# A mixture-of-experts stage on one core: another order of turns between single large experts and pairs of small ones

## The chip, the cores and the metric

The kernel runs on one core of a Trainium2 chip. The metric is device time in microseconds (us), the median of several executions. It has 2298.35 us before the change (three executions, 2296.97 to 2299.94).

## What is computed

Two transformer-like blocks over 256 tokens of width 1024. All but the last part stays as it is. The change touches only the last mixture of experts: 8 experts, each a SwiGLU of inner width 2816, two experts for each token.

```python
N_EXPERTS_2, TOP_K, D_EXPERT = 8, 2, 2816

def swiglu(t, w_gate, w_up, w_down):
    return (jax.nn.silu(t @ w_gate) * (t @ w_up)) @ w_down

def moe_swiglu(h, w_router, w_gate, w_up, w_down):
    t = h.reshape(bsz * seq, d)
    ...
    gates = jnp.sum(jax.nn.one_hot(top_idx, N_EXPERTS_2, dtype=jnp.float32) * top_w[..., None], axis=1)
    out = jnp.zeros_like(t)
    for e in range(N_EXPERTS_2):
        out = out + gates[:, e:e + 1].astype(t.dtype) * swiglu(t, w_gate[e], w_up[e], w_down[e])
    return out.reshape(bsz, seq, d)
```

## The kernel before

At run time the experts are ranked by how many tokens they have. Ranks 0 to 3 are the large experts: each is worked on alone, with up to 128 tokens in its rows. Ranks 4 and 5 make one pair and ranks 6 and 7 the other; each pair shares the 128 rows, 64 for either expert. A large expert is item 0, 1, 2 or 3 of the table `STEPS`; the pairs are items 4 and 5. `HEAVY = 4` parts the two kinds.

An item has four steps. Steps 0, 1 and 2 are chunks of the inner width (1024, 1024 and 768 columns): the gate product, the up product, and silu(gate) times up. Step `OUT` (3) is the product with the down weights. Each engine has its own instruction stream and walks through `STEPS` in the same order (`ranked_pe`, `ranked_act`, `ranked_experts_dve`, and `sync`, which issues the loads), so the one table sets the order of everything.

All weights come once from HBM, in units of two rows of the contraction index: 128 x 2048 float32, 1.049 MB, or three quarters of that in step 2. They go into the ring `fine`, which has 8 slots. SyncE loads unit u as soon as unit u - 8 is released (`Ring.load`, L139), strictly in order of `STEPS`. A step needs these units:

- large expert: 8 in steps 0 and 1, 8 of three quarters in step 2 (6 full ones in bytes), 11 in `OUT`
- pair: twice as many (16, 16, 16 of three quarters, 22), and always two slots together, one of each expert.

The two kinds use a unit differently. A large expert's weights are split into a high and a low part in fp32r: ScalarE casts to `w_hi` (L192, `make_hi`), VectorE subtracts to `w_lo` (L202, `make_lo`), in parts of 1024 columns with four buffers (`PARTS`), and TensorE makes three products of each (L263 to L265). The slot is released when the last `w_lo` of the unit is made, up to four parts ahead of TensorE. A pair's weights are multiplied straight from the slot in float32 (L2476 for gate and up, L2532 for down), and both slots are released when TensorE has done with them.

Between the products lie a few other steps. `mid_pe` (L2269) turns the middle result of the step before, behind the gate product of the next step. `scatter_pe` (L252) adds a finished item's rows back to the tokens; it waits for the chain `y_gated` (VectorE, L2418), `ysb_hi` (ScalarE, L2351), `ysb_lo` (VectorE, L2424). `heavy_end` says how far ScalarE and VectorE may split ahead: to the end of the uninterrupted run of steps of large experts.

Of the kernel before, what the change touches and what calls it, by code (L numbers as in the profile page):

```python
# [301 lines left out]
def row_parts(n, kt=KD):  # L302
# [13 lines left out]
HEAVY = 4  # L316
RANKS = {0: (0,), 1: (1,), 2: (2,), 3: (3,), 4: (4, 5), 5: (6, 7)}
OUT = 3
STEPS = ((0, 0), (0, 1), (4, 0), (0, 2), (0, OUT), (4, 1), (1, 0), (1, 1), (4, 2), (1, 2), (1, OUT), (4, OUT),
         (2, 0), (2, 1), (5, 0), (2, 2), (2, OUT), (5, 1), (3, 0), (3, 1), (5, 2), (3, 2), (3, OUT), (5, OUT))  # L320
INS = [step for step in STEPS if step[1] != OUT]
OUTS = [i for i, ch in STEPS if ch == OUT]

# [6 lines left out]
def heavy_after(i, ch):  # L330

    n = STEPS.index((i, ch)) + 1
    return next((step for step in STEPS[n:] if step[0] < HEAVY), None)


def heavy_end(i, ch):

    n = STEPS.index((i, ch))
    while n + 1 < len(STEPS) and STEPS[n + 1][0] < HEAVY:
        n += 1  # L340
# [3743 lines left out]
```

## Time and profile before

| what | before |
|---|---|
| median of three executions | 2298.35 us |
| profiled execution, its own time | 2297.53 us |
| its span in the trace | 2295.7 us |
| TensorE busy | 1971.2 us (86%) |
| VectorE busy, ScalarE busy | 1088.6 us, 852.2 us |
| weights of the last experts (264 units of 1.049 MB) | 277 MB |

The last experts take about the last 690 us of the span. In this text a "run" is a series of steps of large experts with no pair between them. DMA rates are those of all 16 engines together. TensorE's rows overlap each other by pipelining, so its busy share is no measure of how near it is to its peak.

### The profile page before, as it was taken

The page shows a single profiled execution, that of the slowest core. Times are in us where ns is not written, and L with a number is a line of the kernel's source. Part 1 is how long each engine was busy: PE and PEld are TensorE (multiplying, and loading weights), DVE is VectorE, ACT ScalarE, POOL GpSimd, SP SyncE. Part 2 cuts the span into 40 slices and gives each one's busy share as a digit, 9 for nine tenths or more (in the row PEclk, how much of TensorE's full clock was granted, in tenths as well). Part 3 has the DMA queues.
Part 4 walks back from the last instruction along what each step waited for, and adds up shares of the span by engine and source line. Part 5 has one row for each costly group of instructions (what it writes and reads, how often), then busy time and mean ns, then how long its engine had stood idle before and what let it go on. Part 6 is the DMA issues. An engine that isn't in the chain of part 4 may idle for free.

```text
span 2295.7 us, 29235 instructions
## 1 busy us (share of the span) xinstructions
PE 1971.2 (86%) x12057; PEld 1404.6 (61%) x12057; DVE 1088.6 (47%) x1665; ACT 852.2 (37%) x1153; POOL 43.7 (2%) x109
## 2 busy tenths in 40 slices
PE   6989997996666666698999999999989998999996
PEld 6968776762211211256899898878575674674672
DVE  3845555431111110223555477866484572573571
ACT  4432345310000000234444357855363452463460
POOL 0010200000000000000000000000000000000000
PEclk9989999999777888899999999998999999999999
DMA  8463562579999999849455544405999999999996
GB/s 266 174 220 111 200 233 75 208 296 394 409 409 409 409 409 409 326 174 370 159 183 184 201 130 160 167 5 227 384 390 387 390 408 409 389 407 409 381 408 274
DMA packets 227524, 663.02 MB, mean 289 GB/s; under 512 B 20101, under 2 KB 28841, under 8 KB 227125
## 3 DMA queue, kind: packets, MB, share of 16 engines
q1 hardware_dynamic: 219628, 652.92, 74.4%
q10 hardware_dynamic: 7752, 8.11, 1.2%
q8 instruction: 99, 1.62, 0.3%
q14 instruction: 45, 0.36, 0.1%
HBM read 659.90 MB, written 1.10 MB: 288 GB/s over the span
## 4 chain that ended last, share of the span: by engine, by line
PE 53%; DMA 23%; DVE 13%; ACT 7%; issue 3%; POOL 0%; ACTq 0%; SPq 0%; DVEq 0%; POOLq 0%
PE psum L263 11%; PE psum L265 11%; PE psum L264 11%; PE psum L252 6%; DMA ring<-in_w_expert_down 5%; DMA ring<-in_w_expert_up 5%; DMA ring<-in_w_expert_gate 5%; PE psum L2476 4%; DMA ring<-in_moe_w_gate 3%; DVE w_lo L202 3%; PE psum L2773 2%; ACT w_hi L192 2%; DMA ring<-in_moe_w_down 2%; PE psum L2532 2%; PE psum L1184 1%
## 5 line engine op out<-in xcount | busy, mean ns | idle before, releaser
L202 DVE TENSOR_TENSOR w_lo<-ring,w_hi 128x1024 fp32r<-128x1024 f32 (+1 forms) x498 | 579.6, 1187 | 415.0 <-ACT w_hi L192 406.6
L192 ACT CAST w_hi<-ring 128x1024 fp32r<-128x1024 f32 (+1 forms) x498 | 501.0, 1020 | 390.4 <-PE psum L265 286.5
L2773 PE MATMUL psum<-ring,hT 128*32 128x512 f32 x960 | 158.7, 796 | 104.3 <-DMA ring<-in_w_expert_gate 58.7
L2773 PEld LDWEIGHTS psum<-ring,hT 128*32 128x32 f32 x960 | 31.2, 129 | 224.7 <-issue 100.9
L2476 PE MATMUL psum<-ring,xg_pair 128*64 128x512 f32 (+1 forms) x768 | 156.5, 559 | 13.3 <-DMA ring<-in_moe_w_up 13.3
L263 PE MATMUL psum<-w_hi,xg_hi 128*128 128x512 f32 (+1 forms) x384 | 148.1, 386 | 17.5 <-DVE w_lo L202 17.4
L2379 DVE TENSOR_TENSOR x<-x,psum 128x1024 f32<-128x1024 f32 x26 | 31.2, 1219 | 253.1 <-PE psum L252 253.1
L265 PE MATMUL psum<-w_lo,xg_hi 128*128 128x512 f32 (+1 forms) x384 | 145.8, 380 | 0.0
L264 PE MATMUL psum<-w_hi,xg_lo 128*128 128x512 f32 (+1 forms) x384 | 145.8, 380 | 0.0
L2476 PEld LDWEIGHTS psum<-ring,xg_pair 128*64 128x64 f32 x768 | 55.5, 137 | 108.9 <-issue 105.8
L2795 PE MATMUL psum<-ring,midT 128*32 128x512 f32 x480 | 69.8, 716 | 41.6 <-DMA ring<-in_w_expert_down 41.1
L263 PE MATMUL psum<-h_f_hi,w_hi 128*128 128x256 f32 x352 | 100.6, 286 | 1.5 <-DVE h_f_lo L895 1.5
L264 PE MATMUL psum<-h_f_hi,w_lo 128*128 128x256 f32 x352 | 100.4, 285 | 0.0
L265 PE MATMUL psum<-h_f_lo,w_hi 128*128 128x256 f32 x352 | 100.3, 285 | 0.0
L263 PEld LDWEIGHTS psum<-w_hi,xg_hi 128*128 128x128 f32 x384 | 73.5, 191 | 39.0 <-DVE w_lo L202 13.4
L2532 PE MATMUL psum<-ring,midT 128*64 128x512 f32 x352 | 79.3, 596 | 12.2 <-DMA ring<-in_moe_w_down 12.2
L265 PEld LDWEIGHTS psum<-w_lo,xg_hi 128*128 128x128 f32 x384 | 73.2, 191 | 14.5
L264 PEld LDWEIGHTS psum<-w_hi,xg_lo 128*128 128x128 f32 x384 | 73.4, 191 | 13.9
L259 PE MATMUL psum<-ident 128*128 128x128 f32 x582 | 73.5, 285 | 0.0
L263 PE MATMUL psum<-w_hi,midT_hi 128*128 128x512 f32 x176 | 70.3, 399 | 3.0 <-DVE w_lo L202 3.0
L259 PEld LDWEIGHTS psum<-ident 128*128 128x128 f32 x582 | 71.1, 201 | 2.1 <-issue 1.6
L263 PE MATMUL psum<-h_mix_hi,w_hi 128*128 128x256 f32 x224 | 63.1, 282 | 7.8 <-DVE w_lo L202 7.8
(694 smaller groups left out, 3676.7 us busy)
## 6 DMA issues: line engine op xcount, KB each, us to landing
ring<-in_moe_w_down SPq DMA_DIRECT2D x88, 1024.0 KB, 14.2
ring<-in_w_expert_gate SPq DMA_DIRECT2D x32, 2048.0 KB, 17.6
ring<-in_moe_w_gate SPq DMA_DIRECT2D x64, 1024.0 KB, 12.9
ring<-in_moe_w_up SPq DMA_DIRECT2D x64, 1024.0 KB, 12.7
ring<-in_w_expert_down SPq DMA_DIRECT2D x30, 2048.0 KB, 17.0
ring<-in_w_expert_up SPq DMA_DIRECT2D x28, 2048.0 KB, 17.4
ring<-in_ada_w SPq DMA_DIRECT2D x24, 2048.0 KB, 11.7
ring<-in_moe_w_gate SPq DMA_DIRECT2D x32, 768.0 KB, 11.1
```

The source lines that it names most:

```text
L192: a.copy(self.buffers(n, src.shape)[0], src).then_inc(*self.hi_made.up())
L202: v.tensor_tensor(lo, src, hi.bitcast(F32), SUB).then_inc(*self.lo_made.up())
L252: ins = p.matmul(o, l, r, start=n == 0, stop=n == len(terms) - 1)
L259: p.matmul(o[:, 0:P], constant[:, :], constant[:, :], start=True, stop=True)
L263: p.matmul(o, l[0], r[0], start=start, stop=False)
L264: p.matmul(o, l[1], r[0], start=False, stop=False)
L265: return p.matmul(o, l[0], r[1], start=False, stop=stop)
L2379: v.tensor_tensor(M.acc[:, t, :], M.acc[:, t, :], run.banks.of(st.name, "scatter", i, t), ADD).then_inc(*st.dve.up("acc", i, t))
L2476: ins = p.matmul(ps[r, cut], moe2.xg_pair[:, i - HEAVY, k0 + k, r], w[side][:, k, cut], start=k0 + k == 0, stop=k0 + k == KD - 1)
L2532: ins = p.matmul(ps[r, cut], M.midT[:, k0 + k, r], w[side][:, k, cut], start=first, stop=last)
L2773: ins = p.matmul(ps[slots_of(j), g * 512:(g + 1) * 512], M.xg[:, 2 * q + k, slots_of(j)], w[:, j, k, :], start=2 * q + k == 0, stop=2 * q ...
L2795: ins = p.matmul(ps[slots_of(j), cut], M.midT[:, q, slots_of(j)], w[:, j, cut], start=q == 0, stop=q == 3)
```

## The change

Only the last two thirds of the table `STEPS` change. Nothing is added or removed; the same products, splits and loads come in another order.

```diff
-STEPS = ((0, 0), (0, 1), (4, 0), (0, 2), (0, OUT), (4, 1), (1, 0), (1, 1), (4, 2), (1, 2), (1, OUT), (4, OUT),
-         (2, 0), (2, 1), (5, 0), (2, 2), (2, OUT), (5, 1), (3, 0), (3, 1), (5, 2), (3, 2), (3, OUT), (5, OUT))
+STEPS = ((0, 0), (0, 1), (4, 0), (0, 2), (0, OUT), (4, 1), (1, 0), (4, 2), (1, 1), (1, 2), (1, OUT), (4, OUT),
+         (2, 0), (5, 0), (2, 1), (5, 1), (2, 2), (2, OUT), (3, 0), (5, 2), (3, 1), (3, 2), (3, OUT), (5, OUT))
```

Up to (1, 0) both orders are the same, and the order in which the items end (`OUTS`) stays as well. In ScalarE's stream, at the third pair step (4, 2), `w_hi` is the split of a large expert's weights, `hT` the silu, and `midT` the turned middle result (`midT_hi` for a large expert). The difference reads:

```order
 L2582 COPY midT<-psum 128x1024
-L192 CAST w_hi<-ring 128x1024 x16
-L2602 ACTIVATE hT<-psum 128x1024
-L2582 CAST midT_hi<-psum 128x1024
 L192 CAST w_hi<-ring 128x1024 x4
 L2602 ACTIVATE hT<-psum 128x768
 L2582 CAST midT_hi<-psum 128x1024
+L192 CAST w_hi<-ring 128x1024 x12
+L2602 ACTIVATE hT<-psum 128x1024
+L2582 COPY midT<-psum 128x768
```

The silu of the pair's chunk (128x768) now follows one chunk of expert 1, and the second chunk of expert 1 comes behind it.

The second place is the end of expert 2 in VectorE's stream. `total` is `y_gated`, `x` the addition to the tokens, `selg` the selection of the next item's rows, `ada_row` the middle result. Before, the end of expert 2 is followed by a pair, (5, 1):

```order
L202 TENSOR_TENSOR w_lo<-ring,w_hi 128x1024 x16
L2418 SCALAR_TENSOR_TENSOR total<-psum,slot_gate,gate_b 128x1024
L2424 TENSOR_TENSOR ysb_lo<-total,ysb_hi 128x1024
L2379 TENSOR_TENSOR x<-x,psum 128x1024 x2
L202 TENSOR_TENSOR w_lo<-ring,w_hi 128x1024
L2674 TENSOR_TENSOR ada_row<-hT,psum 128x1024
L202 TENSOR_TENSOR w_lo<-ring,w_hi 128x1024 x3
L2648 TENSOR_SCALAR selg<-slots,ranked 128x128 x2
```

Now it is followed by a large expert's chunk, (3, 0), with the pair (5, 2) behind that:

```order
L202 TENSOR_TENSOR w_lo<-ring,w_hi 128x1024 x20
L2418 SCALAR_TENSOR_TENSOR total<-psum,slot_gate,gate_b 128x1024
L2424 TENSOR_TENSOR ysb_lo<-total,ysb_hi 128x1024
L2648 TENSOR_SCALAR selg<-slots,ranked 128x128 x2
L202 TENSOR_TENSOR w_lo<-ring,w_hi 128x1024 x8
L2379 TENSOR_TENSOR x<-x,psum 128x1024 x2
L202 TENSOR_TENSOR w_lo<-ring,w_hi 128x1024 x4
```

Four more parts are split ahead (20, not 16), and the chain of `y_gated` and `ysb_lo` now stands between splits that TensorE needs at once.

## Rows read from the trace of the kernel before

**Rows 1.** The page: span, and busy time of each engine

```profile
span 2295.7 us, 29235 instructions
PE 1971.2 (86%) x12057; PEld 1404.6 (61%) x12057; DVE 1088.6 (47%) x1665; ACT 852.2 (37%) x1153; POOL 43.7 (2%) x109
```

**Rows 2.** Windows of the last stage: busy us by engine, clock, DMA share, GB/s

```profile
1705.00:1740.00 35.00, 35.00 (x157) 21.87 (x157) 19.73 (x17) 13.96 (x14) 0.00 (x0) 1.00 0.91 343
1740.00:1800.00 60.00, 56.85 (x256) 38.25 (x253) 40.06 (x36) 35.64 (x35) 0.00 (x0) 1.00 1.03 409
1800.00:1820.00 20.00, 20.00 (x114) 11.50 (x114) 5.42 (x6) 3.93 (x5) 0.00 (x0) 1.00 0.95 361
1820.00:1925.00 105.00, 98.94 (x488) 61.27 (x486) 52.06 (x58) 42.19 (x50) 0.00 (x0) 1.00 1.03 407
...
1985.00:2000.00 15.00, 15.00 (x71) 5.80 (x71) 1.22 (x1) 0.00 (x0) 0.00 (x0) 1.00 0.85 332
...
2065.00:2100.00 35.00, 31.21 (x139) 12.71 (x137) 5.99 (x5) 2.07 (x2) 0.00 (x0) 1.00 1.03 409
...
2150.00:2165.00 15.00, 15.00 (x89) 7.55 (x89) 1.22 (x1) 1.78 (x2) 0.00 (x0) 1.00 0.87 313
```

**Rows 3.** Waits of SyncE's DMA queue, 1650 to 2296: total us, times, longest

```profile
SPq L139 <- DVE w_lo L202: 270.9, 124, 6.1
```

**Rows 4.** Chain that ended last, 1590 to 2296: start, us, what

```profile
1650.78 13.31 DMA ring<-in_moe_w_up
...
1727.07 13.88 PE psum L2476 x64
...
1757.27 1.05 ACT w_hi L192
...
1761.89 0.50 PE psum L263
...
1807.21 10.47 PE psum L2476 x64
...
1830.30 0.84 ACT w_hi L192
...
1833.91 0.50 PE psum L263
...
1883.33 7.02 PE psum L2532 x32
...
1932.20 1.05 ACT w_hi L192
...
1939.22 0.50 PE psum L263
...
1939.99 0.43 PE psum L265
...
1987.02 13.88 PE psum L2476 x64
...
2015.70 0.84 ACT w_hi L192
...
2019.74 0.50 PE psum L263
...
2069.38 13.88 PE psum L2476 x64
...
2102.49 1.05 ACT w_hi L192
...
2107.11 0.51 PE psum L263
...
2152.50 10.47 PE psum L2476 x64
```

**Rows 5.** VectorE's timeline at the end of expert 2

```profile
2069.42 1.28 DVE L2418 SCALAR_TENSOR_TENSOR total<-psum,slot_gate,gate_b 128x1024 f32<-128x1024 f32 x1 [3.28 <-PE psum L265]
2071.81 1.22 DVE L2424 TENSOR_TENSOR ysb_lo<-total,ysb_hi 128x1024 fp32r<-128x1024 f32 x1 [1.11 <-ACT ysb_hi L2351]
```

## Prediction

> **What bounds the kernel now.** I read the page first. TensorE is busy 86% of the span [rows 1], which invites the thought that TensorE is the limit. The windows of the last stage correct that: DMA moves 407 to 409 GB/s wherever nothing holds it up, with its share at its top value [rows 2]. At that rate a unit of 1.049 MB takes 1.049 / 0.409 = 2.56 us, so the 264 units of the last experts need 676 us of a stage of about 690. The stage is bound by transfers, with TensorE close behind, and the only time that another order can win or lose is time in which DMA has nothing to fetch because all 8 slots are taken.
>
> The windows show such stretches, always where a pair's step begins: 343 GB/s in 1705 to 1740, 361 in 1800 to 1820, 332 in 1985 to 2000, 313 in 2150 to 2165 [rows 2]. In lost time, length x (1 - rate / 409), these are 5.6, 2.3, 2.8 and 3.5 us. The first lies ahead of the changed part. The other three, at (4, 2), (5, 0) and (5, 2), sum to 8.7 us (I add the unrounded values). They are what the change can remove at the very most: 0.38% of the time.
>
> Why there? The chain of waits gives the pace of each kind [rows 4]. A large expert's chunk takes TensorE 22.7 us: two of them lie between 2107.11 and 2152.50. Its loads take 8 x 2.56 = 20.5. So DMA gains 2.2 us on TensorE in each chunk, plus the head start at a run's beginning. On a pair the sign is the other way: 64 rows of L2476 take 13.88 us for four double units, 3.5 us each, against 5.1 us of loading. A pair's step lets TensorE catch up and wait. SyncE's queue waits for `w_lo` 270.9 us in all, 124 times [rows 3], but most of that is an ordinary full queue with loads in flight; only the windows tell when it cost anything.
>
> **A rule for the stall.** Take as zero the time when the first unit of a run starts to load (its landing in rows 4 minus its own transfer). DMA runs dry when it has loaded the run and the first 8 units of the pair behind it. It gets a slot again when TensorE has done the pair's first double unit. The margin M is the second time minus the first. From rows 4:
>
> - (4, 2): zero at 1757.27 - 2.56 = 1754.7. DMA dry at + 16 x 2.56 + 8 x 1.92 = 1811.1. TensorE starts the pair at 1807.2, + 2.6 for three-quarter units. M = -1.3, measured stall 2.3.
> - (5, 0): zero 1932.20 - 2.56 = 1929.6, dry at + 24 x 2.56 = 1991.1, TensorE 1987.0 + 3.5. M = -0.6, stall 2.8.
> - (5, 2): zero 2099.9, dry at 2156.3, TensorE 2152.5 + 2.6. M = -1.2, stall 3.5.
> - (4, 1): zero 1650.78 + 13.31 = 1664.1, dry at + 25 x 2.56 = 1728.1, TensorE 1727.1 + 3.5. M = +2.5, stall 5.6.
> - (4, OUT): zero 1830.30 - 1.92 = 1828.4, dry at 1892.4, TensorE 1883.3 + 3.5. M = -5.6, no stall: 407 GB/s [rows 2].
> - (5, 1): zero 2013.8, dry at 2077.8, TensorE 2069.4 + 3.5. M = -4.9, no stall: 409 GB/s [rows 2].
>
> The stall is M + k with k of 3.1 to 4.7, and zero where that is negative. I read k as the issue of new loads, the time until they deliver at full rate, and the thinning out of the last ones; the rows give only its sum. I take k = 3.5, and 4.7 for (5, 2), which showed it. The Trainium skill ("DMA: Bandwidth & Descriptors", section "Anatomy of one DMA") gives a fixed part of about 2.0 us for each transfer; taken alone as k it would be an estimate about 1.5 us smaller at each stall, and the measured k speaks for more than that.
>
> **The change, place by place.** The new runs are: (1, 0) alone; (1, 1), (1, 2), (1, OUT); (2, 0) alone; (2, 1) alone; (2, 2), (2, OUT), (3, 0); (3, 1), (3, 2), (3, OUT). In units the old ones were 16, 17, 16, 17, 16, 17; the new ones are 8, 25, 8, 8, 25, 25. Runs are halved where they were short, and three of them grow to 25.
>
> - *(4, 2) behind (1, 0).* TensorE's start was +52.5 and comes 22.7 earlier, at +29.8, + 2.6; dry at 20.5 + 15.4 = 35.9. M = -3.5, and with k = 3.5 nothing is left; with k = 4.7 it is 1.2, the bound. Gain 2.3.
> - *(4, OUT) behind 25 units.* First matmul of the run: the first unit's 2.56 plus the 4.6 from landing to matmul (1757.27 to 1761.89). Then 22.7 for (1, 1) and 49.4 for (1, 2) and (1, OUT) (1833.91 to 1883.33). TensorE starts the pair at +79.3, + 3.5. Dry at 20.5 + 43.6 + 20.5 = 84.6. M = -1.8, stall 1.7. Loss 1.7; bounds 0 and 3.
> - *(5, 0) behind (2, 0).* Before, run start to pair start was 57.4; without (2, 1) it is 34.7, + 3.5; dry at 41.0. M = -2.8, stall 0.7. Gain 2.1.
> - *(5, 1) behind (2, 1).* First matmul +7.2, chunk 22.7, + 3.5 = 33.4 against 41.0. M = -7.6: no stall, and none before.
> - *(5, 2) behind (2, 2), (2, OUT), (3, 0).* First matmul +5.9 (2013.8 to 2019.74); (2, 2) and (2, OUT) 49.6 (2019.74 to 2069.38). Then (3, 0): 22.7, about 1.0 more for the scatter in the place of a turned middle, and a new wait. For the first time a large expert's `OUT` is followed by a large expert's chunk. Four parts are split ahead; that covers TensorE for 4 x 1.4 = 5.6 us (22.7 / 16 a part). But the fourth can be cast only when the last part of `OUT` is used: its two steps take about 2.2, then `y_gated` 1.28, `ysb_hi` about 1.1, `ysb_lo` 1.22 [rows 5], `selg` about 0.6, and the fifth `w_lo` 1.2, in all 7.6. Two us are not covered. Were the fourth part early, nothing would be; that is the lower bound. So (3, 0) takes 25.7, the pair starts at +81.2, + 2.6; dry at 15.4 + 28.2 + 20.5 + 15.4 = 79.5. M = +4.3, and with k = 4.7 the stall is 9.0 against 3.5 now. Loss 5.5; bounds 2 (no uncovered wait, k 3.1: 5.4) and 7.
> - *(5, OUT) behind 25 units.* As (4, OUT): loss 1.7; bounds 0 and 3.
>
> Sum: -2.3 + 1.7 - 2.1 + 5.5 + 1.7 = +4.5 us. The end itself does not move otherwise: (5, OUT) is a pair's step and ends on its last transfer in both orders. Against the profiled execution (own time 2297.53, 1.8 above the span) it gives 2302.0; its own time is 0.8 below the median, so measured medians should stand at 2298.35 + 4.5, about 2302.9.
>
> **The rivals.** A measurement of this kernel can tell 0.2%, 4.6 us, from no change; the forecast lies at that edge.
>
> *Within the noise (24%).* The long runs cost their lead and no more: no uncovered wait at (3, 0), k at its low end, (4, OUT) and (5, OUT) hidden as today. Stalls 5.4 instead of 8.7: -3.3, about 2295. For it: VectorE waits 3.28 us for TensorE ahead of `y_gated` [rows 5], so it has time in hand. Against: those four parts are capped by the buffers.
>
> *Faster (11%).* One mechanism: the stall comes from two whole chunks ahead of a pair, not from the length of a run. Runs that end in `OUT` stand ahead of (4, OUT) and (5, 1) without a stall, and if that holds for 25 units the stalls at (4, 2) and (5, 0) go with nothing in their place: -5.1, or -8.7 (2289.6) if (5, 2) is free too. It decides when the three long runs together add under 0.5 us. Against it is (4, 1): a run with `OUT`, M above zero, 5.6 us lost.
>
> *Much slower (13%).* TensorE loses its clock more often. At 1939.99 a matmul takes 0.43 us [rows 4], after the gap from the landing at 1932.20; at 22.7 / 96 = 0.24 us a matmul normally, some nine such rows cost about 1.8 us. After the shorter gap at 1757 the chain goes on at full pace, and the windows show 1.00. In the new order pairs follow each other sooner, so TensorE waits for loads through more of each pair's step. Were each of three new run starts to cost 1.8 us and pass it on to the stall behind it, the time would be 2308.3. The Trainium skill ("TensorE: Matmul & The Clock Gate", section "HAM oscillation — how this bites in real kernels") describes just such a kernel, half clock after each wait for DMA. The trace agrees for the long gap at 1932 only.
>
> **How the numbers follow.** The forecast's own case (52%) reaches from +1.5 to +8, where the bounds above put it: 2300 to 2306. The range must take in the quiet case and most of the slow one: 2295.5 to 2309. Chances: faster by over 0.2%, the 11% and a sliver of the quiet case, 12%. Slower by over 0.2%, all 13% and, since +4.5 lies at the edge, rather more than half of my main case, 33%: 46%. The rest, 42%, is within 0.2%.
>
> **What would show it.** In the windows of the changed kernel DMA stays above 400 GB/s at the starts of (4, 2) and (5, 1). It falls well below at (5, 2), for about 9 us in lost time, which is the largest loss behind (1, 0). Small losses stand at (4, OUT) and (5, OUT). Between (2, OUT) and (3, 0) TensorE waits about 2 us for `w_lo` about 5 us into the chunk. It would be wrong if (5, 2) starts with a ring that still has loads in flight, or if rows of 0.43 us come at the new run starts.

## The result, and the profile after

The changed kernel takes 2303.94 us (median of 9 executions, 2299.69 to 2307.91); the kernel before took 2297.47 in the same series (9 executions). The ratio is 1.0029, with a 95% interval of 1.0020 to 1.0037: slower by about 6.5 us. The forecast was 2302.9 with a range of 2295.5 to 2309.0, or 4.5 us slower.

The time before the last experts varies by several us from one execution to the next: TensorE's first pair starts between 1632.95 and 1641.17 us in the profiles of this study. So spans say little here, and the profiled execution of the changed kernel (2299.69 us) is also the fastest of its nine. I compare the stage itself, from the start of TensorE's first pair, (4, 0), to the end of its last matmul of weights. These four rows are the two ends in the chain of waits, of the kernel before and then of the changed one; the columns are start, us, what.

```profile
1636.38 13.91 PE psum L2476 x64
...
2276.37 3.67 PE psum L2532 x16
```

```profile
1632.95 13.88 PE psum L2476 x64
...
2278.54 3.67 PE psum L2532 x16
```

The stage takes 2280.04 - 1636.38 = 643.7 us before and 2282.21 - 1632.95 = 649.3 after: 5.6 us more, which is the change of the median within its interval. From here on "the stage" is this stretch.

The windows of the changed kernel answer to [rows 2]. Last column: GB/s; the one ahead of it: DMA's busy share.

```profile
1780.00:1800.00 20.00, 18.26 (x111) 8.14 (x111) 2.44 (x2) 1.82 (x2) 0.00 (x0) 1.00 1.03 401
1800.00:1880.00 80.00, 75.92 (x362) 60.31 (x359) 64.99 (x61) 56.26 (x59) 0.00 (x0) 0.98 1.03 407
1880.00:1910.00 30.00, 30.00 (x144) 13.21 (x144) 7.48 (x15) 3.19 (x5) 0.00 (x0) 1.00 0.95 369
...
1960.00:1980.00 20.00, 20.00 (x96) 7.93 (x96) 2.44 (x2) 2.03 (x2) 0.00 (x0) 1.00 0.98 383
1980.00:2045.00 65.00, 57.65 (x260) 30.36 (x256) 22.35 (x19) 20.00 (x20) 0.00 (x0) 1.00 1.03 409
...
2115.00:2140.00 25.00, 25.00 (x121) 17.59 (x121) 15.96 (x14) 9.78 (x10) 0.00 (x0) 1.00 0.77 270
...
2230.00:2255.00 25.00, 25.00 (x114) 11.33 (x114) 8.15 (x12) 1.64 (x2) 0.00 (x0) 1.00 0.95 375
```

The reader is to look for the rates under 407 and turn each into lost time, length x (1 - rate / 409):

| pair's step | before | forecast | after |
|---|---|---|---|
| (4, 2) | 2.3 | 0 | 0.4 |
| (4, OUT) | 0 | 1.7 | 2.9 |
| (5, 0) | 2.8 | 0.7 | 1.3 |
| (5, 1) | 0 | 0 | 0 |
| (5, 2) | 3.5 | 9.0 | 8.5 |
| (5, OUT) | 0 | 1.7 | 2.1 |
| sum, us | 8.7 | 13.1 | 15.2 |

The difference, 6.5 us, is as large as the change of the median; the stage of the two profiled executions grew by 5.6. Added up over the whole stage, in windows of 5 us, the lost time goes from 24.8 to 30.2 us, which is 5.4 more and fits the stage. That the six places alone give just the 6.5 of the median is partly luck.

The chain of the changed kernel answers to [rows 4]. These are the run starts and the pair starts behind them.

```profile
1753.81 1.05 ACT w_hi L192
...
1758.43 0.50 PE psum L263
...
1780.51 10.47 PE psum L2476 x64
...
1805.59 1.05 ACT w_hi L192
...
1809.94 0.79 PE psum L263
1810.74 0.43 PE psum L264
...
1883.53 7.02 PE psum L2532 x32
...
1929.38 1.05 ACT w_hi L192
...
1962.26 13.88 PE psum L2476 x64
...
2133.56 10.47 PE psum L2476 x64
2144.03 1.02 PE psum L2269 x8
...
2157.17 1.05 ACT w_hi L192
...
2235.10 7.02 PE psum L2532 x32
```

At (4, OUT) the run's first load lands at 1805.59, so the zero of the margin is 1803.0. DMA's dry point is 1803.0 + 84.6 = 1887.6, TensorE gives the first slots back at 1883.53 + 3.5: M = -0.6, and the loss of 2.9 means k = 3.5. The other places are read in the same way below.

The new wait at the junction of (2, OUT) and (3, 0) is the one row that the old trace could not have. First TensorE's row of the timeline, then VectorE's.

```profile
2114.68 0.47 PE L263 MATMUL psum<-w_hi,xg_hi 128*128 128x512 f32 x1 [2.07 <-DVE w_lo L202]
```

```profile
2106.78 2.57 DVE L202 TENSOR_TENSOR w_lo<-ring,w_hi 128x1024 fp32r<-128x1024 f32 x2 [0.23 <-ACT w_hi L192]
2109.27 1.28 DVE L2418 SCALAR_TENSOR_TENSOR total<-psum,slot_gate,gate_b 128x1024 f32<-128x1024 f32 x1
2111.66 1.23 DVE L2424 TENSOR_TENSOR ysb_lo<-total,ysb_hi 128x1024 fp32r<-128x1024 f32 x1 [1.11 <-ACT ysb_hi L2351]
2112.80 0.60 DVE L2648 TENSOR_SCALAR selg<-slots,ranked 128x128 f32<-128x128 f32 x2
2113.31 6.90 DVE L202 TENSOR_TENSOR w_lo<-ring,w_hi 128x1024 fp32r<-128x1024 f32 x6
```

VectorE makes no `w_lo` between 2109.35 and 2113.31, so the fifth part is ready only at about 2114.5. TensorE took up the first of its four parts in store at 2107.0, and they last to 2112.61; from there it waits.

### The profile page after: what moved, and what is told of

The parts are those of the page before. It is cut to its first block, busy times and chain, and to the rows that moved or that the text cites. A ratio compares the mean times of both kernels' runs of the same rounds, so it can differ in the third digit from the quotient of the medians.

```text
span 2297.9 us, 29235 instructions
## 1 busy us (share of the span) xinstructions
PE 1957.1 (85%) x12057; PEld 1402.4 (61%) x12057; DVE 1088.9 (47%) x1665; ACT 852.4 (37%) x1153; POOL 43.5 (2%) x109
## 4 chain that ended last, share of the span: by engine, by line
PE 55%; DMA 22%; DVE 13%; ACT 7%; issue 3%; POOL 0%; ACTq 0%; SPq 0%; DVEq 0%; POOLq 0%
PE psum L263 11%; PE psum L264 11%; PE psum L265 11%; PE psum L252 6%; DMA ring<-in_w_expert_down 5%; DMA ring<-in_w_expert_up 5%; DMA ring<-in_w_expert_gate 5%; PE psum L2476 4%; DMA ring<-in_moe_w_gate 3%; DVE w_lo L202 3%; PE psum L2773 2%; PE psum L2532 2%; ACT w_hi L192 2%; DVE xbc L983 1%; PE psum L1184 1%
## 5 line engine op out<-in xcount | busy, mean ns | idle before, releaser
L2773 PE MATMUL psum<-ring,hT 128*32 128x512 f32 x960 | 146.1, 740 | 117.9 <-DMA ring<-in_w_expert_gate 64.6
L2476 PE MATMUL psum<-ring,xg_pair 128*64 128x512 f32 (+1 forms) x768 | 156.9, 560 | 16.7 <-DMA ring<-in_moe_w_up 14.6
L2773 PEld LDWEIGHTS psum<-ring,hT 128*32 128x32 f32 x960 | 30.2, 125 | 227.0 <-issue 89.0
## 6 DMA issues: line engine op xcount, KB each, us to landing
ring<-in_moe_w_gate SPq DMA_DIRECT2D x32, 768.0 KB, 13.1
```

Source lines behind the costliest of these rows:

```text
L2476: ins = p.matmul(ps[r, cut], moe2.xg_pair[:, i - HEAVY, k0 + k, r], w[side][:, k, cut], start=k0 + k == 0, stop=k0 + k == KD - 1)
L2773: ins = p.matmul(ps[slots_of(j), g * 512:(g + 1) * 512], M.xg[:, 2 * q + k, slots_of(j)], w[:, j, k, :], start=2 * q + k == 0, stop=2 * q ...
```

## Experiments

Each kernel was timed in the same series as the kernel before, and its ratio is to that one. Where a diff shows the table `STEPS`, the line taken away is that of the changed kernel.

**Only expert 1 reordered.** It asks whether the three groups cost alike.

```diff
-         (2, 0), (5, 0), (2, 1), (5, 1), (2, 2), (2, OUT), (3, 0), (5, 2), (3, 1), (3, 2), (3, OUT), (5, OUT))
+         (2, 0), (2, 1), (5, 0), (2, 2), (2, OUT), (5, 1), (3, 0), (3, 1), (5, 2), (3, 2), (3, OUT), (5, OUT))
```

> Only expert 1 gets the new order, (1, 0), (4, 2), (1, 1), (1, 2), (1, OUT), (4, OUT); experts 2 and 3 keep the old one. Theory of the margin: the stall at (4, 2) goes from 2.3 to about 0.4 us, one of about 3.0 appears at (4, OUT), the stalls at (5, 0) and (5, 2) stay at 2.8 and 3.5; in sum about +1 us against the kernel before. Rival, each run of 25 units costs a like share of what the whole change cost (6.5 us over three such runs): +2.2 us. Rival, the loss has nothing to do with this group: 0 or a gain of 2.

Measured: 2296.20 us against 2297.13, ratio 0.9995 (0.9984 to 1.0005). The stage takes 643.6 us, as before. Two windows of its trace, at (4, 2) and at (4, OUT):

```profile
1800.00:1820.00 20.00, 14.91 (x75) 8.84 (x76) 8.15 (x8) 7.42 (x8) 0.00 (x0) 1.00 1.03 406
1885.00:1905.00 20.00, 20.00 (x95) 8.95 (x95) 7.20 (x14) 2.12 (x3) 0.00 (x0) 1.00 0.95 367
```

The loss of 2.3 at (4, 2) is gone, and 2.1 have come at (4, OUT). The group is neutral. A like share for every long run is refuted: 2.2 us, ratio 1.0010, lies beyond the interval.

**Only experts 2 and 3 reordered.**

```diff
-STEPS = (..., (1, 0), (4, 2), (1, 1), (1, 2), (1, OUT), (4, OUT),
+STEPS = (..., (1, 0), (1, 1), (4, 2), (1, 2), (1, OUT), (4, OUT),
```

> Only experts 2 and 3 get the new order. Theory of the margin: (5, 0) 1.3 us of lost transfer time instead of 2.8, (5, 2) 8.5 instead of 3.5, (5, OUT) 2.1 instead of 0, (4, 2) still 2.3: in sum about +5.5 us against the kernel before. Rival, equal share for each run of 25 units: +4.3 us. Whichever, the windows should show one large loss, ahead of and at (5, 2).

Measured: 2303.58 us against 2297.13, ratio 1.0028 (1.0017 to 1.0039), stage 649.0. This half makes the whole loss. Its own windows show 305 GB/s in 2115 to 2155, 10.2 us at (5, 2), where 8.5 was forecast: one large loss, and not a like share for each long run. Seven matmuls at 0.43 us (half clock; 0.23 us at full clock) stand in the run ahead of it, behind the new wait, which the changed kernel's profiled execution does not have there.

```profile
2115.00:2155.00 40.00, 37.91 (x181) 25.56 (x181) 22.21 (x22) 16.25 (x17) 0.00 (x0) 0.96 0.85 305
```

**The new wait taken away.** In the changed kernel one more part is split between the halves of the chain.

```diff
             for k0 in range(0, M.n_k, M.kout):
                 lo_after(v, i, OUT, out_unit(i, k0))
+            if heavy_end(i, OUT) != (i, OUT):
+                y_gated_dve(v, run2, i, run2.multiplied(out_unit(i)))
+                fine_split.make_lo(v, fine_split.end(out_unit(i)) + PARTS + 1)
+                y_lo_dve(v, run2, i)
+                return
...
             for k0 in range(0, M.n_k, M.kout):
                 hi_after(a, i, OUT, out_unit(i, k0))
+            if heavy_end(i, OUT) != (i, OUT):
+                fine_split.make_hi(a, fine_split.end(out_unit(i)) + PARTS + 1)
```

> The changed kernel, but at the end of expert 2 a fifth part is cast and subtracted between the two halves of the chain y_gated, ysb_hi, ysb_lo. Theory: TensorE's wait of 2.1 us inside (3, 0) goes, (5, 2) starts 2.1 us earlier and its stall falls from 8.5 to about 6.4: 2 us faster than the changed kernel, some 4.4 slower than before. Rival, the wait is hidden because DMA has loads in flight then: the wait goes and the stall at (5, 2) and the time stay as in the changed kernel.

Measured: 2301.01 us against 2297.13, ratio 1.0011 (1.0001 to 1.0022); stage 647.6, 1.7 less than the changed kernel. TensorE's waits in 2100 to 2125:

```profile
PE psum L263 <- DVE w_lo L202: 0.6, 1, 0.6
```

2.07 us of waiting have become 0.6, and at (5, 2) the windows show 321 GB/s in 2115 to 2150, a loss of 7.5 instead of 8.5, where 6.4 was forecast. The wait does pass on to the end, so the rival that it is hidden falls. Between 1.0 us (the windows) and 1.7 us (the stage) of the loss were this wait. The intervals of this kernel and the changed one overlap, so it is the trace that carries this, not the medians.

**The pair ahead of (3, 0).** No junction of two large experts, but a run of 33 units.

```diff
-         ... (2, 2), (2, OUT), (3, 0), (5, 2), (3, 1), (3, 2), (3, OUT), (5, OUT))
+         ... (2, 2), (2, OUT), (5, 2), (3, 0), (3, 1), (3, 2), (3, OUT), (5, OUT))
```

> The changed order with (5, 2) moved ahead of (3, 0): runs of 8, 25, 8, 8, 17 and 33 units. It takes away the junction of a large expert's down product with a large expert's chunk. Theory of the margin: (5, 2) behind 17 units has M = 5.9 + 49.6 + 2.6 - 59.0 = -0.9 and loses 2.6 to 3.8 us; (5, OUT) behind 33 units has M = 6.9 + 45.4 + 49.4 + 3.5 - 105.1 = +0.1 and loses 3.2 to 4.8 us; with 3.4 at expert 1 and 1.3 at (5, 0) about 11.7 in sum, 3 us slower than before and 3 faster than the changed kernel. Rival, a run's length alone sets the loss: 33 units lose more than the 8.5 us of 25, and the kernel is 7 us or more slower than before.

Measured: 2297.88 us against 2297.13, ratio 1.0003 (0.9994 to 1.0013); stage 646.7, 3.0 more than before and 2.6 less than the changed kernel. The windows at (5, 2) and at (5, OUT):

```profile
2100.00:2125.00 25.00, 25.00 (x127) 15.96 (x126) 11.54 (x10) 8.73 (x9) 0.00 (x0) 1.00 0.90 340
...
2210.00:2255.00 45.00, 44.25 (x199) 28.02 (x199) 28.21 (x30) 18.26 (x18) 0.00 (x0) 1.00 0.96 369
```

They lose 4.2 and 4.4 us; the forecasts were 2.6 to 3.8, which was a little too low, and 3.2 to 4.8. The longest run of all loses half of what 25 units lost ahead of (5, 2), so length alone does not set the loss. The median is 2 us better than the stage makes one expect.

**An order with one short run.** It keeps the short run (2, 0), without a junction of two large experts.

```diff
-STEPS = (..., (1, 0), (4, 2), (1, 1), (1, 2), (1, OUT), (4, OUT),
-         (2, 0), (5, 0), (2, 1), (5, 1), (2, 2), (2, OUT), (3, 0), (5, 2), (3, 1), (3, 2), (3, OUT), (5, OUT))
+STEPS = (..., (1, 0), (1, 1), (4, 2), (1, 2), (1, OUT), (4, OUT),
+         (2, 0), (5, 0), (2, 1), (2, 2), (2, OUT), (5, 1), (3, 0), (5, 2), (3, 1), (3, 2), (3, OUT), (5, OUT))
```

> An order between the two: (1, 0), (1, 1), (4, 2), (1, 2), (1, OUT), (4, OUT), (2, 0), (5, 0), (2, 1), (2, 2), (2, OUT), (5, 1), (3, 0), (5, 2), (3, 1), (3, 2), (3, OUT), (5, OUT): runs of 16, 17, 8, 25, 8, 25 units, and no large expert's chunk behind a large expert's down product. Theory: stalls of 2.3 at (4, 2), 1.3 at (5, 0), 1.7 to 3 at (5, 1), 0.4 at (5, 2), 2 at (5, OUT), in sum about 8 against 8.7: the same as before within 0.1%. Rival, each run of 25 units costs 2.2 us net: 4 us slower than before.

Measured: 2292.79 us against 2298.70, ratio 0.9979 (0.9966 to 0.9991): faster than before. The stage takes 640.5, 3.2 less. Its two runs of 25 units stand ahead of (5, 1) and (5, OUT):

```profile
2070.00:2085.00 15.00, 15.00 (x70) 5.26 (x68) 2.51 (x2) 1.04 (x1) 0.00 (x0) 1.00 0.98 382
2110.00:2150.00 40.00, 37.31 (x200) 23.25 (x198) 14.51 (x13) 12.62 (x13) 0.00 (x0) 1.00 1.03 403
2228.00:2253.00 25.00, 25.00 (x115) 10.13 (x115) 6.42 (x10) 1.04 (x1) 0.00 (x0) 1.00 0.95 378
```

They lose 1.0 and 1.9, and (5, 2) behind (3, 0) alone next to nothing. With 2.4 at (4, 2) and 0.5 at (5, 0) that is 6 of lost time, against 8.7. I had forecast the same time as before; the theory's direction was right and its size too small. The medians stand 5.9 us apart, and the stage of the two profiles shows only 3.2 of that.

**The clock.** 16 products of a constant ahead of three run starts, in the changed kernel.

```diff
+                if (i, ch) in ((1, 1), (2, 0), (3, 1)):
+                    constant_products(p, ps, ident, 16)
```

> The changed kernel with 16 idle products of a constant ahead of the first matmul of (1, 1), (2, 0) and (3, 1), where its trace shows 5, 14 and 6 matmuls at 0.43 us. Their results are overwritten. Theory of the clock as a part of the loss: these rows fall to 0.24, the pairs behind come 1.2, 2.8 and 1.2 us earlier, and the stalls at (4, OUT), (5, 0) and (5, OUT) lose about 1.2, 1.3 and 1.2: 3 to 4 us faster than the changed kernel. Rival, the clock is no part of it: same time as the changed kernel; or the products come too late and delay the run: slower by up to 3.

Measured: 2304.94 us against 2298.70, ratio 1.0031 (1.0019 to 1.0043); stage 649.1, 0.2 less than the changed kernel. The granted clock at the three starts is 1.00:

```profile
1810.00:1820.00 10.00, 10.00 (x65) 8.03 (x62) 6.82 (x7) 6.10 (x6) 0.00 (x0) 1.00 1.02 407
1935.00:1950.00 15.00, 14.36 (x79) 11.05 (x76) 12.14 (x13) 10.22 (x11) 0.00 (x0) 1.00 1.03 410
2160.00:2170.00 10.00, 9.24 (x61) 7.26 (x62) 5.59 (x6) 5.04 (x5) 0.00 (x0) 1.00 1.03 410
```

The cure worked and the time stayed. From the landing to the pair's start (5, 0) gained 2.8 us and its loss went; the other two gained 0.7 and 0.4, and their losses stayed at 3.0 and 2.6 us. My 3 to 4 us were wrong. But the products have a price of their own. At (1, 1) the first `w_lo` is ready at 1814.41, and TensorE comes to it at 1815.62, when the products are done:

```profile
1812.03 3.84 PE L259 MATMUL psum<-ident 128*128 128x128 f32 x32
1813.18 1.23 DVE L202 TENSOR_TENSOR w_lo<-ring,w_hi 128x1024 fp32r<-128x1024 f32 x1 [12.66 <-ACT w_hi L192]
1815.62 0.47 PE L263 MATMUL psum<-w_hi,xg_hi 128*128 128x512 f32 x1
```

At (3, 1) the delay is 1.6 us (2165.51 to 2167.08). So this run shows that the cure as it stands wins nothing; what half clock alone costs at these two starts stays open.

**Seven slots instead of eight**, in both kernels.

```diff
-    fine = Ring(fine_t, semaphore, "fine", 2 * SLOTS)
+    fine = Ring(fine_t, semaphore, "fine", 7)
```

> The changed kernel with 7 slots instead of 8 in the ring of the last experts; everything else as it is. Theory: DMA runs dry one unit earlier at every pair's step, 2.56 us, or 1.92 behind which three-quarter units stand. That adds 2.6 each at (4, 0), (4, 1), (4, OUT), (5, 0), (5, OUT), 1.9 each at (4, 2) and (5, 2), nothing at (5, 1) (M = -7.6): +16.8 us against the changed kernel, 23 against the kernel before. Rival, the loss at (5, 2) is TensorE's own waiting and the slots are no part of it: a few us at most.

> The kernel before with 7 slots instead of 8. Theory: 2.6 each at (4, 0), (4, 1), (5, 0), 1.9 each at (4, 2) and (5, 2); (4, OUT), (5, OUT) and (5, 1) have M of -5.6, -5.6 and -4.9 and begin to lose 0.5, 0.5 and 1.2: +13.8 us. So the two orders should stand about 9 us apart with 7 slots, more than the 6 to 7 with 8, since the new order has more places at the brink. Rival as for the other kernel: a few us at most.

Measured, in one series: 2320.04 us with the new order and 2308.68 with the old, against 2297.97; ratios 1.0104 (1.0089 to 1.0120) and 1.0049 (1.0032 to 1.0066). The new order loses 22.1 us against the kernel before (forecast 23), the old one 10.7 (forecast 13.8). The stages take 666.4 and 651.2: +17.1 and +7.5 where the theory has 16.8 and 13.8. The direction and the first size hold, and the two orders now stand 11 us apart instead of 6 to 7 (forecast 9). That the stage of the old order grows by only half of the forecast is not explained. Its profiled execution, 2302.52 us, is 6.2 us faster than its median, and the medians give 10.7. At (5, 2), where the forecast has 3.5 + 1.9 = 5.4, its trace shows 340 GB/s over 25 us, a loss of 4.2.

**Half units**, 16 slots of one row each, in both kernels.

```diff
-        self.kper = KD if self.step <= 512 else 2
-        self.kout = 4 if self.step <= 512 else 2
+        self.kper = KD if self.step <= 512 else 1
+        self.kout = 4 if self.step <= 512 else 1
...
-    fine_t = ring_t[:, :, :].rearrange("p s (h n) -> p (s h) n", h=2)
-    fine = Ring(fine_t, semaphore, "fine", 2 * SLOTS)
+    fine_t = ring_t[:, :, :].rearrange("p s (h n) -> p (s h) n", h=4)
+    fine = Ring(fine_t, semaphore, "fine", 4 * SLOTS)
...
```

> The changed kernel with the ring of the last experts cut into 16 slots of one row each instead of 8 of two; the same bytes and the same room. Theory: a pair gives a slot back after 1.75 us instead of 3.5 and the large experts' slots come free one part sooner, so each of the stalls of the last stage shrinks by 1.7 us or so ((4, 0), (4, 1), (4, OUT), (5, 2), (5, OUT); the small ones go), and the tail behind the last transfer is 1.8 us shorter: 8 to 10 us faster than the changed kernel, 2 to 4 faster than before. Rival, twice as many transfers pay a fixed cost each that shows: not faster, or slower, and the rate in the windows without a stall falls below 409 GB/s.

> The same finer ring on the kernel before. Theory: stalls at (4, 0), (4, 1), (4, 2), (5, 0), (5, 2) lose about 1.7 us each and the tail 1.8: 8 to 10 us faster than before, so the two orders stay about 5 us apart, or come somewhat closer as small stalls go to zero. Rival as for the finer ring on the changed kernel: no gain or a loss.

Measured, in one series: 2299.52 us with the new order and 2288.39 with the old, against 2298.70; ratios 1.0006 (0.9996 to 1.0016) and 0.9953 (0.9936 to 0.9970). The old order with the finer ring is 10.3 us faster than before, its stage 8.6 shorter. Added up over the whole stage, its lost time is 16.7 us where the kernel before has 24.8, so nearly all of the gain is DMA running dry for a shorter time. With the changed kernel the stage is only 3.3 shorter, and its largest loss does not shrink. The windows of the finer ring with the new order, at two points ahead of (5, 2) and then over all of that place:

```profile
2080.00:2085.00 5.00, 2.85 (x8) 2.01 (x7) 5.00 (x7) 3.67 (x4) 0.00 (x0) 0.76 1.02 406
...
2115.00:2120.00 5.00, 3.97 (x11) 3.12 (x12) 4.77 (x5) 2.82 (x3) 0.00 (x0) 0.67 0.97 355
2115.00:2145.00 30.00, 28.97 (x132) 19.85 (x134) 17.48 (x15) 11.11 (x11) 0.00 (x0) 0.94 0.77 259
```

259 GB/s over 30 us is a loss of 11.0, against 8.5. TensorE's clock fell twice within this one run, at the turn of the middle result and at the new wait (the columns read 0.76 and 0.67). So the forecast for the old order held, and that for the new one failed. Whether the dips alone made the difference was not tried.

**Half units with one short run.** The table with one short run, and the finer ring.

> The order with only two long runs (16, 17, 8, 25, 8, 25 units) together with 16 slots of half a unit. Theory: the gain of the order (0.21%) and that of the finer ring (0.47%) are of the same lost transfer time; with the finer ring the stalls left behind (4, 1) in the old order are about 1 us, so the order adds little: 0 to 2 us faster than the finer ring alone, 10 to 12 faster than before. Rival, they add up: 16 us faster than before. Rival, the long runs cost more on the finer ring, as in the changed kernel: only 6 to 8 faster.

Measured: 2289.45 us against 2297.97, ratio 0.9964 (0.9950 to 0.9978): 8.5 us faster, where 10 to 12 was forecast, and no better than the finer ring with the old order. The two gains do not add. The kernel before with half units has the lowest median of this study, 2288.39 us, though its interval overlaps that of this kernel.

## Why the prediction held

**The bound.** Transfers bind the last stage, and an order can win or lose only where DMA runs dry. This held: the lost time of the whole stage grew by 5.4 us, the stage by 5.6. The forecast of the change was 2.0 us too small (+4.5 for +6.5).

**Where the loss sits.** (5, 2) behind (2, 2), (2, OUT), (3, 0), forecast 9.0 us, measured 8.5. In its terms: the run's first load lands at 2053.31, so the zero is 2051.4. TensorE starts the pair at +82.2 (forecast +81.2). M is +5.3 (forecast +4.3), and k 3.2, where I had taken 4.7. The margin was 1.0 too small and k 1.5 too large, and the two errors hid each other, so that 9.0 came so close to 8.5 is partly luck. The load's landing is where ScalarE's wait for it ends:

```profile
2053.31 1.57 ACT L192 CAST w_hi<-ring 128x768 fp32r<-128x768 f32 x2 [16.60 <-DMA ring<-in_moe_w_gate]
```

Of the 1.0, 0.8 lies in (3, 0), which took TensorE 26.5 us (2107.0 to 2133.56) and not 25.7. What k consists of was not tested. The fixed part of 2.0 us that the prediction set beside it is told in the Trainium skill ("DMA: Bandwidth & Descriptors", section "Anatomy of one DMA") of transfers issued from GpSimd, and here SyncE issues them.

**The new wait.** Forecast 2.0 us, measured 2.07; removing most of it moved the pair and the stall by 1.5 and 1.0.

**Why this place and not the other long runs.** Three parts meet here. TensorE's run is 25 units with a scatter in it, the new wait lies inside, and the loads of the pair behind are three-quarter units. A slot counts units, not bytes. Eight of these are on the way in 15.4 us, not 20.5, so DMA is dry 5.1 us sooner than at (4, OUT). The order with one short run shows the reverse: 25 units ahead of full units lose 1.0 and 1.9, and the three-quarter units behind a run of 8 almost nothing. No run changes the size of the units alone, so the 5.1 us are worked out and not measured. The rate shows how it happens. In 2125 to 2130 it is 182 GB/s, before the pair begins at 2133.56: slots come back at best at the pace of TensorE's full units, 2.84 us each (22.7 / 8), and each brings a load of only 0.79 MB, 277 GB/s at best.

```profile
2115.00:2120.00 5.00, 5.00 (x23) 4.08 (x22) 5.00 (x5) 3.33 (x4) 0.00 (x0) 1.00 1.03 390
2120.00:2125.00 5.00, 5.00 (x23) 4.00 (x22) 4.82 (x5) 3.28 (x4) 0.00 (x0) 1.00 0.99 357
2125.00:2130.00 5.00, 5.00 (x23) 4.04 (x22) 4.60 (x5) 3.17 (x3) 0.00 (x0) 1.00 0.55 182
```

SyncE's own rows say the same. These are the first 16 loads of (5, 2), of the kernel before and then of the changed one:

```profile
2128.94 20.84 SPq L139 DMA_DIRECT2D ring<-in_moe_w_gate  x8
2155.27 8.93 SPq L139 DMA_DIRECT2D ring<-in_moe_w_up  x8
```

```profile
2106.71 24.14 SPq L139 DMA_DIRECT2D ring<-in_moe_w_gate  x8
2136.33 8.63 SPq L139 DMA_DIRECT2D ring<-in_moe_w_up  x8
```

The pause between the rows, when all slots are taken, is 5.5 us in both. But the eight loads ahead of it go out in 24.1 us instead of 20.8, so DMA has less in flight when the pause begins.

**The smaller terms.** (4, OUT) was put at 1.7 and lost 2.9, the term most mis-sized. The run behind (4, 2) starts with half-clock rows that I had kept for the rival, and its pair starts at 1883.53 - 1803.0 = +80.5, not +79.3. (5, 0) lost 1.3 for 0.7, (4, 2) 0.4 for 0, (5, OUT) 2.1 for 1.7. Together these added 2.6 and (5, 2) took back 0.5: +6.5 or so for +4.5.

**The rivals.** "Within the noise" fell with the wait and the 8.5 us. "Faster", that two whole chunks make the stall and not a run's length, fell with (4, OUT). "Much slower" had its mechanism: matmuls at 0.43 us came at (1, 1), (2, 0) and (3, 1). The prediction had named just this as a sign that it would be wrong, and it came true at (1, 1) and (3, 1) without the slow case; it was a poor sign. The price was smaller than thought: the time stayed inside the main case, and keeping the clock up bought 0.2 us of the stage, net of the products' own delay. The Trainium skill ("TensorE: Matmul & The Clock Gate", section "HAM oscillation — how this bites in real kernels") has half clock after waits for DMA; the trace agrees in part, since the start of (1, 0), at 1758, stayed at full clock. Nor does the length of the gap sort them, as the prediction had it: from the landing to that row 4.6 us pass (1753.81 to 1758.43), and at (1, 1), with half clock, only 4.3 (1805.59 to 1809.94). The trace before, too, has rows of 0.43 us at a second place, from 1675.83 on, in (0, 2), which the prediction overlooked.

## What to carry to other kernels

When transfers bind and the order of work is free, write down for each run of slow-to-release work the margin between "TensorE gives a slot back" and "all slots are loaded"; the stall is that margin plus 2.7 to 4.7 us here. That is no sharper than a microsecond: with the same margin of -0.6, (4, OUT) lost 2.9 and (5, OUT) 2.1. Halving a run below its break-even wins nothing more, and the work taken from it makes another run longer, which pays in full. A ring whose slots count units holds less time when the units are small, and a finer ring can buy more than a new order: 0.47% against 0.21% here. It did so with the old order only; with the changed one it bought about half.

## What was not expected of the hardware

TensorE's granted clock falls in different places in different executions of nearly the same program. Behind the new wait of 2 us it stayed at 1.00 in the changed kernel, and with experts 2 and 3 alone reordered seven matmuls took 0.43 us. The loss at (5, 2) was 8.5 us in the one and 10.2 in the other, whose order there is the same; that the dip made this difference is likely but was not tried.
